# The output products of two state-space heads: wide ones side by side, then the narrow ones, behind one wait

## The reference

```python
def ssd_chunked(xdt, adt, bmat, cmat):
    ...
    y_diag = jnp.einsum("bcgls,bgrcls,bcsgrp->bclgrp", cb, decay_in, X)
    ...
    y_off = jnp.einsum("bclgn,bcgrpn,bgrcl->bclgrp", Cc, states, jnp.exp(a_cum))
    return (y_diag + y_off).reshape(b, l, h, p)
```

## Time and profile before

| | us |
|---|---|
| median of three runs (3432.72 to 3437.0) | 3434.11 |
| the profiled execution's own time | 3438.93 |
| its span, first to last instruction | 3437.1 |
| PE busy | 3053.4 (89%) |
| DVE busy | 2252.5 (66%) |
| ACT busy | 1730.1 (50%) |
| POOL busy | 67.2 (2%) |
| mean granted clock of PE | 0.929 |

### The profile page before, as it was taken

How to read it: one execution, slowest core, us unless ns; L and a number is a source line. 1 busy time by engine, 2 the same in 40 slices (tenths; PEclk the granted TensorE clock), 3 DMA queues, 4 the chain that set the end, 5 groups by cost and what they waited for, 6 DMA issues and landing times.

```text
span 3437.1 us, 57540 instructions
## 1 busy us (share of the span) xinstructions
PE 3053.4 (89%) x22901; PEld 2806.8 (82%) x22901; DVE 2252.5 (66%) x2670; ACT 1730.1 (50%) x1852; POOL 67.2 (2%) x68
## 2 busy tenths in 40 slices
PE   6988889979969878899889788988669999999997
PEld 6987888969959878788879686977359999998996
DVE  3559995754545589966555454554338888888887
ACT  4444449334434444384344443443226666666665
POOL 0000003000000000020000000000000000000000
PEclk9998889989989989899999898998569999999999
DMA  6543232435545533233445452544028999999996
GB/s 186 183 153 111 87 99 99 139 127 188 183 131 183 177 98 100 74 111 123 157 155 187 139 174 98 183 154 164 0 86 298 348 321 321 321 339 347 321 321 225
DMA packets 485898, 619.95 MB, mean 180 GB/s; under 512 B 31841, under 2 KB 436211, under 8 KB 485747
## 3 DMA queue, kind: packets, MB, share of 16 engines
q1 hardware_dynamic: 485747, 617.90, 54.5%
HBM read 616.81 MB, written 1.05 MB: 180 GB/s over the span
## 4 chain that ended last, share of the span: by engine, by line
PE 73%; DVE 15%; issue 7%; ACT 4%; DMA 1%; SPq 1%; DVEq 0%; ACTq 0%
PE PS L636 11%; PE PS L583 11%; PE PS L584 10%; PE PS L585 10%; PE PS L856 4%; PE PS L858 4%; PE PS L857 4%; PE PS L1017 2%; PE PS L1018 2%; PE PS L1019 2%; DVE w_lo L1500 2%; ACT w_hi L1092 2%; PE PS L905 1%; ACT w_hi L1431 1%; PE PS L886 1%
## 5 line engine op out<-in xcount | busy, mean ns | idle before, releaser
L1500 DVE TENSOR_TENSOR w_lo<-raw,w_hi 128x2048 fp32r<-128x2048 f32 x313 | 711.3, 2288 | 420.8 <-ACT w_hi L1092 419.8
L583 PE MATMUL PS<-x_hi,w_hi 128*128 128x256 f32 x3360 | 974.3, 290 | 11.3 <-DVE x_lo L1512 4.8
L584 PE MATMUL PS<-x_hi,w_lo 128*128 128x256 f32 x3360 | 965.3, 287 | 0.0
L585 PE MATMUL PS<-x_lo,w_hi 128*128 128x256 f32 x3360 | 964.5, 287 | 0.0
L1092 ACT ACTIVATE w_hi<-raw 128x2048 fp32r<-128x2048 f32 x313 | 597.9, 1910 | 424.5 <-PE PS L636 281.4
L583 PEld LDWEIGHTS PS<-x_hi,w_hi 128*128 128x128 f32 x3360 | 660.4, 197 | 22.9 <-issue 7.5
L584 PEld LDWEIGHTS PS<-x_hi,w_lo 128*128 128x128 f32 x3360 | 660.7, 197 | 1.9
L585 PEld LDWEIGHTS PS<-x_lo,w_hi 128*128 128x128 f32 x3360 | 659.8, 196 | 0.0
L856 PE MATMUL PS<-w_hi,x_hi 128*128 128x256 f32 x1488 | 429.3, 288 | 9.8 <-DVE x_lo L2119 8.1
L858 PE MATMUL PS<-w_lo,x_hi 128*128 128x256 f32 x1488 | 422.1, 284 | 0.0
L857 PE MATMUL PS<-w_hi,x_lo 128*128 128x256 f32 x1488 | 422.1, 284 | 0.0
(11 more groups left out here) (397 smaller groups left out, 4286.0 us busy)
## 6 DMA issues: line engine op xcount, KB each, us to landing
raw<-in_w_gu_moe_dram SPq DMA_DIRECT2D x98, 1024.0 KB, 8.4
XC<-in_w_gu_moe_dram SPq DMA_DIRECT2D x80, 1024.0 KB, 8.9
raw<-in_w_in_dram SPq DMA_DIRECT2D x64, 1024.0 KB, 5.8
raw<-in_w_down_moe_dram SPq DMA_DIRECT2D x48, 1024.0 KB, 8.4
raw<-in_ffn_w_gate_dram SPq DMA_DIRECT2D x44, 1024.0 KB, 5.3
raw<-in_ffn_w_up_dram SPq DMA_DIRECT2D x44, 1024.0 KB, 6.9
raw<-in_ffn_w_down_dram SPq DMA_DIRECT2D x44, 1024.0 KB, 5.1
G<-in_w_down_moe_dram SPq DMA_DIRECT2D x40, 1024.0 KB, 8.7
```

The costliest lines, as they stand in the source:

```text
L583: mm(dst, w_hi[:, slot, w0:w0 + P], hi, start=start, stop=False, skip_group_check=True)
L584: mm(dst, w_lo[:, slot, w0:w0 + P], hi, start=False, stop=False, skip_group_check=True)
L585: return mm(dst, w_hi[:, slot, w0:w0 + P], lo, start=False, stop=True, skip_group_check=True)
L1500: tt(w_lo[:, slot, :], raw[:, slot, :], w_hi[:, slot, :].bitcast(F32), SUB)\
```

## The change

In each step the two waits for `masked`, one ahead of each head, become one wait for both. The order of the four products becomes wide of head 0, wide of head 1, narrow of head 0, narrow of head 1, where it was wide and narrow of head 0, then wide and narrow of head 1. Operands, destinations and flags of every product are the same, and so is their number.

```diff
                 for u in range(2):
                     if i >= 1:
                         pe.wait_ge(s["y_ready"], n.due("y_ready"))
-                    for hh in range(2):
-                        pe.wait_ge(s["masked"], n.due("masked"))
-                        o, w = 64 * hh, xt[:, i % 2, :]
-                        d = decay[:, i % 2, 2 * u + hh, :]
-                        mm(PS[o:o + 64, 6 + u, 0:T], w[:, u * P + o:u * P + o + 64], d[:, 0:T],
-                           start=True, stop=True, skip_group_check=True)
-                        last = mm(PS[o:o + 64, 6 + u, P:T], w[:, T + u * P + o:T + u * P + o + 64], d[:, T:T + P],
-                                  start=False, stop=True, skip_group_check=True)
+                    pe.wait_ge(s["masked"], n.due("masked", 2))
+                    w = xt[:, i % 2, :]
+                    for tokens, keys, wide in ((slice(0, T), 0, slice(0, T)), (slice(P, T), T, slice(T, T + P))):
+                        for hh in range(2):
+                            o = 64 * hh
+                            last = mm(PS[o:o + 64, 6 + u, tokens], w[:, keys + u * P + o:keys + u * P + o + 64],
+                                      decay[:, i % 2, 2 * u + hh, wide], start=(keys == 0), stop=True, skip_group_check=True)
                     last.then_inc(s["y_psum"], n.one("y_psum"))
```

## The result

The changed kernel takes 3442.4 us (median of 11 runs, 3435.8 to 3445.3) against 3434.1 us (11 runs, 3432.5 to 3437.7): a ratio of 1.0021, with a 95% interval from 1.0011 to 1.0030. It is slower by 8 us where 3 were forecast, and lies above the stated range of 3431.5 to 3440.5 us. The profiled execution took 3444.69 us with a span of 3442.9, that is 5.8 us more than the profiled one of before.

The account below looks back on a forecast made before the run. PE's own work was taken to set the pace; -0.5 us for the lag, 0 for the waits and +3.4 for the tails' clock gave +2.9: 3441.8 us profiled, 3437.0 us median, range 3431.5 to 3440.5 us.

Parts of the forecast that it names:

- What bounds the kernel: Steady blocks: PE's own work sets the pace, and the two heads of a step already run beside each other.
- third rival: Steady blocks ran in program order, so side-by-side issue would save 0.7 us each, 8.4 us in all: 3425.7 us, chance 0.03.
- rival of the lost overlap: Heads no longer overlap in the new order, 1.4 us lost per steady block, tails too: 3456.9 us, chance 0.04.
- rival of the late pair: Tail's pair does not overlap when its mask comes last, +1.3 us per layer's last step: 3439.6 us, chance 0.06.
- The waits in the steady blocks: One wait for both masks costs nothing there, since the last mask is ready 3.2 us before its block.
- the lag: Second head trails 0.04 us more in a steady block's second step; removing it in 12 blocks wins 0.5 us.
- The clock at the tail: New pause of about 1.1 us between tail steps keeps PE's clock at 0.50 longer: 1.7 us lost per layer.
- The sum: Whole kernel: -0.5 us, 0 for the waits and 3.4 us for the tails' clock give +2.9 us.
- clock stretches elsewhere that shift by a step either way: Clock changes outside the tails, given no term in the forecast time; chance 0.05.
- The step from one profile to the median: Whole kernel: median taken as 4.8 us below the profiled execution, as before the change, turning 3441.8 into 3437.0 us.
- The range: Whole kernel: 3431.5 to 3440.5 us, from 3433.6 less half the runs' spread to 3439.6 and a little more.

Follow-up runs that it names:

- e1: Changed kernel with its one wait for both masks, but the old order of the products: 3441.8 us, ratio 1.0017 to before.
- e3: Change in the seven steady blocks of each layer only, old code in the tail block ssd_output(7): 3434.4 us, ratio 0.9999 to before.
- e2: Changed kernel with its new order of the products, but the two waits of before: 3436.8 us, ratio 1.0005 to before.
- e5: Changed kernel with three extra unused narrow products filling PE's pause between the tail's two steps: 3434.3 us, ratio 1.0002 to before.
- e7: Changed kernel, but at the tail only the first step has the change, the second the old code: 3436.7 us, ratio 1.0003 to before.
- e8: Changed kernel, but at the tail only the second step has the change, the first the old code: 3443.0 us, ratio 1.0022 to before.
- e9: Changed kernel plus 25 extra unused wide products in PE's wait ahead of each layer's second feed-forward part: 3432.8 us, ratio 1.0002 to before.
- e4: Kernel before plus three extra unused wide products behind each layer's tail block, as a delay: 3438.9 us, ratio 1.0013 to before.
- e10: Changed kernel with the tail's pause filled, plus 25 unused wide products in both 12.15 us waits of each layer: 3431.6 us, ratio 0.9994 to before.
- e11: Kernel before plus 25 extra unused wide products in both 12.15 us waits of each layer: 3432.0 us, ratio 0.9995 to before.
- e6: New order in steady blocks, old code at the tail, six extra unused wide products ahead of the tail: 3436.9 us, ratio 1.0009 to before.

## Why the prediction was wrong

**What bounds the kernel, right.** PE's own work sets the pace in the steady blocks; both heads run side by side in the old order. The new order won 0.05 us for a block (1.50 to 1.45), forecast 0.04. The third rival supposed that the old block ran in program order, and gave up half of it, 0.7 us; 0.05 of 1.50 us went, so it is out. The Trainium skill, "TensorE: Matmul & The Clock Gate", Part 3, "Packing small matmuls", has matmuls start and end strictly in program order; the traces disagree, with x4 and x4 in e1 as in the earlier trace rows.

**The rival of the lost overlap, wrong.** Adjacent halves overlap in the steady block, and at the lower clock too: the changed tail's last step has two heads in 1.55 us, where head 2 alone took 595.30 - 593.77 = 1.53 us. With that the rival of the late pair is out as well. The mechanism that the rival named, a queue of loads for each head, no run tested.

**The waits in the steady blocks at nothing, right**: e3 has them and takes 3434.4 us. The cause of the lag is the order (e1, e2).

**The clock at the tail, right in mechanism and size.** Forecast 1.7 us a layer, measured 1.68 and 1.67. The pause came out at 1.38 us, not 1.1, because the first pair had the clock at 1.00 for 0.51 of its 1.07 us (592.09 to the fall at 592.60) and was done sooner. e5, e7 and e8 show the pause as the cause, where the prediction had only a likeness to go by.

**The sum, wrong. This is the step that failed first.** It ended with the tails: "-0.5 for the lag, 0 for the waits and 2 x 1.7 = 3.4 for the clock". Everything behind them was taken to be carried along as it was, and "clock stretches elsewhere that shift by a step either way" got a chance of 0.05. In the profiled execution the tails gave 3.35 us and the starts of the second feed-forward parts 2 x 1.86 = 3.7, less 2 x 0.67 at the ends of the mixers. The knock-on, 2 x 1.2 us net, is the term that was put at nothing; with it the forecast would have been 3439.4 us, in the range, and still 3 us under what was measured. It could have been seen: the timeline before the change had PE idle for 12.15 us ahead of L645 and the clock rising at 777.1, 2.9 us after L645 began; I looked at no stretch behind the group sums. e9 shows that these stretches carry a large part of the loss: with them taken away and the long tail kept, the ratio to before is 1.0002; but its filler also takes away the 10.2 us at 0.50 that before has. That the late tail is what brings the knock-on on goes by the profiles named at e4. What needs no such argument is the whole: every kernel with the pause has a ratio of 1.0017 to 1.0022 (changed, e1, e8; e9 apart), every one without it and without an added delay one that is not clear of 1.

**The step from one profile to the median, too small by 2.5 us.** The two profiled executions differ by 5.8 us, the medians by 8.3. The profiled execution of before lies 4.8 us over its median, that of the changed kernel 2.3 us over its own, and the prediction took the 4.8 off both. The traces show where they lie. e3 keeps time with before through both layers (the last L651 of the second layer at 1747.39 and 1747.72), and its profiled execution, 3434.4 us, is its median and that of before. Behind that point the code is the same, and yet e3 is 3.3 us ahead at the next L651 (2071.36 against 2074.61) and 5.0 us ahead where the second network clears its accumulators (L992 of before, 2684.75 against 2689.74). At the first place before has 20.5 us at 0.50, e3 13.7 and 3.4 us with 3.4 us at 1.00 between them; at the second, before has 3.4 us at 0.50 from 2582.8, e3 none. So the profiled execution of before holds some 4.7 us that its usual execution may well lack. From the last L651 of the second layer to L992 the kernels with a late second layer (changed, e1, e4, e8) take 941.3 to 943.2 us, e2, e3, e5 and e7 take 937.3 to 938.9, and the profiled before 942.0. That reads like a third part of the loss, of some microseconds, in the second network. With one profiled execution for each kernel it is a likeness and not shown; how the 8.3 us divide stays open to that extent. Against the 5.4 us that the forecast of 3437.0 fell short, the knock-on makes 2.4 and this step 2.5.

**The range.** Its upper end, 3440.5 us, took the tail's clock and one more mishap. With the knock-on as a term, and an upper end as far above the forecast as it was (3.5 us), it would have reached 3443, with the measured 3442.4 just inside.

## What to carry to other kernels

One wait in place of two saves nothing where the second is already satisfied, and where it isn't, it takes away work that filled the time in between. When a change moves idle time of PE, look for every place downstream where the clock falls and rises, not only for the next one: a microsecond earlier or later cost 1.6 to 1.9 us more there, in part paid back at another place. Keeping PE at work in one such wait took the stretch at 0.50 behind it away (e9 to e11), even where the gain in time was too small to measure. And one profiled execution is not the median: before a forecast is carried from one to the other, ask which stretches make the difference.

## What the runs showed of the hardware

- Matmuls on the two halves of the output partitions started out of program order: in e1 and before, all four wide ones of a step start ahead of any narrow one, though the second head's stand behind the first head's narrow ones. With eight instructions between the heads a block took 1.50 us (before, e1), with the products side by side 1.45 (changed, e2).
- With a pause of 0.9 to 1.4 us after its fall at the tail, the clock stayed at 0.50 for 6.8 us (changed, e1, e8, e9). With the pause filled it was 3.4 us (e5), and so it was with 3.47 us of idle time ahead of the first step and no pause behind it (e7).
- Matmuls whose result nobody reads, on data or on constants, held the clock at 1.00 through a wait of 12.15 us (e9 to e11) and through the tail (e6, both layers). At the tail that is the weaker case: in the first layer of e4 and of e11 the clock stayed at 1.00 with no such work ahead of it.
- The clock's changes do not move in step with the work: it fell at 766.9 us before and at 766.7 in the changed kernel, whose work was 0.66 us later, and in the second layer at 1732.8 and 1736.1, with work 4.01 us later.
